# 1/rms of the experts' rows from one-hot products, and spare weight units asked for at other points

## The chip, the cores and the metric

The kernel runs on one core of a Trainium2 chip: TensorE (PE, with PEld for its weight loads), VectorE (DVE), ScalarE (ACT), GpSimd (POOL), SyncE (SP, which issues most of the DMA) and 16 DMA engines between HBM and the on-chip memory. The metric is the device time of one execution in microseconds (us).

## The reference, cut to what matters

One decoder layer for 520 tokens (512 of a prompt, 8 of decoding): a mixer, a mixture of experts, a gate. The change touches the experts' input:

```python
u = rmsnorm(h, g_ffn)              # h * (1/rms of h's row) * g_ffn, per token
# router: softmax over 4 groups, top 1; softmax over its 8 experts, top 2
cw = sum(one_hot(eid, 32) * wk)    # two experts of 32 for each token, with weights
for e in range(32):                # D = 1024, D_FF = 512
    t = silu(u @ w_gate[e]) * (u @ w_up[e])
    y = y + cw[:, e:e+1] * (t @ w_down[e])
h = h + y
```

The weights of the 32 experts are 201 MB of float32, and each token uses two experts. The kernel takes only the rows that belong to an expert.

## The kernel before, in words

**The head** (to about 272 us) is a list of TensorE jobs (`JOBS`): the mixer in 128-column pieces of its weights, the output projection (`wo`), transposes of h into rows (`tp`), the router's logits (`lg`), and at the end `rk` (rank of each token in its expert, by triangular products), `ix` and `iy` (for each expert the list of its tokens, by products of one-hot matrices, helper `placed`) and `tot` (rows of each expert). A job's result lies in one of four pairs of PSUM banks and is read by the engines that `READERS` names. Filler products (`spin`, counts in `SPIN`) stand where TensorE would wait.

**h and its 1/rms.** Rows of h go to a DRAM tensor `h_rows` by POOL (`store_rows`, lines 659 and 660, semaphore `h_stored`). A token has two rows there, each with 512 values of h and, behind them, 16 copies of the token's 1/rms (`HR` = 528 values in a row). The copies are made by ACT (`rstd_rows`, line 845) and written by four DMAs of ACT (lines 849 and 850, `rstd_stored`), 1040 pieces of 64 bytes.

**An expert** has a tile of 64 tokens, 128 rows with both halves of h. POOL gathers them with an indirect DMA (`start_gather`, line 676) into `xg`, two buffers in turn. TensorE transposes them (`rows_t`, line 1733), DVE multiplies by the gain (`evac_rows`, line 1383) and copies the 1/rms of each row out of column 512 of `xg` into `rs` (line 1382). TensorE forms gate and up together (`gate_up`, line 1754), ACT and DVE apply silu, `rs` and the product, TensorE transposes (`hidden_t`, line 1762) and multiplies with the down weights (`down`, line 1771). ACT evacuates, and POOL scatters the result to `y_rows` (line 682). Further tiles for an expert with more than 64 tokens exist (`over`), but no such tile runs in these inputs.

**The weights** come in units of 2 MB, three for an expert: unit 0 and 1 for gate and up, unit 2 for down. There are six slots in `arena` and three spare places (`spare[0..2]`) put together from pieces of other buffers that are free by then, in 5, 4 and 8 pieces. SP asks for them in a fixed order, and every request waits in SP's queue for its own condition. Units 0 to 5 go to the slots, unit 6 to spare 0 during the head. Unit 7 goes to spare 1 (line 485) once `h_stored` is complete. Unit 8 goes to spare 2 once the first gather has landed (`xg_loaded[0]`). Unit 9 goes to the slot of unit 0 when the first half of expert 0's `gate_up` is done (`gu_half`, line 546), unit 10 when all of it is done, unit 11 after its `down`, and so on for all that follow.

**The route.** DVE's `rk` step makes `row_hot` (line 1066, float16) and two subtractions for ACT's exponentials (line 854), then `index` (line 1359), which POOL's gather waits for. Behind the last job of the head, DVE computes the weights `wk` (`route_weights`, lines 1072 to 1084, 14 small operations that wait for the exponentials), and then the first `evac_rows`.

**The tail** (from about 743 us): the last scatter, y read back, the gate, the final norm.

## Time and profile before

| | us |
|---|---|
| median of 3 runs (822.83 to 824.47) | 823.37 |
| the profiled execution, its own time | 825.39 |
| its span | 823.6 |

| engine | busy us | share of the span |
|---|---|---|
| PE | 721.8 | 88% |
| DVE | 288.8 | 35% |
| ACT | 179.6 | 22% |
| POOL | 102.6 | 12% |

All rows come from the profiled execution, whose span is 1.8 us shorter than its own time. 258.39 MB move in all. The page's second part cuts the span in 40 slices of 20.6 us. Busy shares are means over stages with different limits, so a stretch is read by its own rows.

### The profile page before, as it was taken

The numbers are of one execution on the slowest core, as the hardware profiler recorded it, in microseconds if no ns is written. First come the engines' busy times: TensorE is split into PE (matmuls) and PEld (weight loads), VectorE is DVE, ScalarE is ACT, GpSimd is POOL, SyncE is SP. The second block draws the span as 40 slices with busy tenths as digits, with TensorE's granted clock in tenths as the row PEclk, the third lists the DMA queues.
The fourth block names the chain that finished last, engine by engine and source line by source line (L and its number), as shares of the span: only waits on it lengthen the run. The fifth ranks groups of instructions, "written<-read, shape, count | busy, mean of one in ns | idle before, by whom it ended". The sixth has DMA issues, their size and how long they took to land.

```text
span 823.6 us, 11299 instructions
## 1 busy us (share of the span) xinstructions
PE 721.8 (88%) x4520; PEld 450.1 (55%) x4520; DVE 288.8 (35%) x520; ACT 179.6 (22%) x274; POOL 102.6 (12%) x161
## 2 busy tenths in 40 slices
PE   8999999999999888999998887777777777778996
PEld 8989999899998433333333222222222222226775
DVE  5556788676434532010111011011001001005875
ACT  7242312233323010011111010000000000004576
POOL 0500000010001112212121211211211111100000
PEclk9999999999999999999999999999999999999999
DMA  9641225663936799999999999999999999995301
GB/s 347 239 181 53 77 80 210 248 224 98 400 132 217 259 409 416 428 426 425 426 425 426 424 427 427 426 425 428 428 424 429 426 427 426 425 422 218 120 27 77
DMA packets 36457, 258.39 MB, mean 314 GB/s; under 512 B 7905, under 2 KB 8465, under 8 KB 22841
## 3 DMA queue, kind: packets, MB, share of 16 engines
q1 hardware_dynamic: 27248, 237.17, 70.3%
q0 software_dynamic: 7072, 19.07, 6.2%
q10 hardware_dynamic: 2096, 1.56, 0.6%
q8 instruction: 31, 0.51, 0.2%
q14 instruction: 10, 0.07, 0.0%
HBM read 251.04 MB, written 15.14 MB: 323 GB/s over the span
## 4 chain that ended last, share of the span: by engine, by line
PE 53%; DMA 36%; DVE 6%; ACT 3%; issue 2%; SPq 0%; DVEq 0%; POOLq 0%; ACTq 0%
DMA arena<-in_w_exp 33%; PE ps L1560 23%; PE ps L1754 15%; PE ps L1771 5%; PE ps L1885 3%; PE ps L1603 1%; DMA region_q<-in_xt 1%; DVE xh L1423 1%; DVE region_u L1376 1%; DMA region_u<-h_rows,index 1%; DMA region_m<-y_rows 1%; PE ps L1568 1%; DMA y_rows<-region_v,both_cols 1%; PE ps L1762 1%; PE ps L1673 0%
## 5 line engine op out<-in xcount | busy, mean ns | idle before, releaser
L1754 PE MATMUL ps<-arena,region_u 128*64 128x512 f32 x960 | 218.3, 600 | 47.0 <-DMA arena<-in_w_exp 46.0
L1754 PEld LDWEIGHTS ps<-arena,region_u 128*64 128x64 f32 x960 | 66.9, 137 | 196.2 <-issue 124.2
L1372 DVE SCALAR_TENSOR_TENSOR region_u<-ps,small,region_u 128x256 f32<-128x256 f32 x32 | 15.5, 484 | 376.7 <-ACT region_u L858 376.7
L1560 PE MATMUL ps<-u_hi,w_hi 128*128 128x260 f32 x448 | 129.2, 288 | 5.1 <-issue 3.3
L1560 PE MATMUL ps<-u_lo,w_hi 128*128 128x260 f32 x448 | 127.4, 284 | 0.0
L1560 PE MATMUL ps<-u_hi,w_low 128*128 128x260 f32 x448 | 127.3, 284 | 0.0
L1771 PE MATMUL ps<-arena,region_u 128*64 128x512 f32 x480 | 109.6, 598 | 6.1 <-DMA arena<-in_w_exp 2.5
L1560 PEld LDWEIGHTS ps<-u_hi,w_hi 128*128 128x128 f32 x448 | 85.1, 190 | 7.0 <-issue 5.0
L1560 PEld LDWEIGHTS ps<-u_hi,w_low 128*128 128x128 f32 x448 | 85.2, 190 | 0.0
L1560 PEld LDWEIGHTS ps<-u_lo,w_hi 128*128 128x128 f32 x448 | 85.2, 190 | 0.0
L682 POOL DMA_INDIRECT y_rows<-region_v,both_cols x32 | 33.3, 1042 | 367.6 <-ACT region_v L862 367.6
L858 ACT ACTIVATE region_u<-ps,small 128x256 f32<-128x256 f32 x32 | 15.1, 473 | 264.3 <-PE ps L1754 264.3
L1771 PEld LDWEIGHTS ps<-arena,region_u 128*64 128x64 f32 x480 | 33.3, 137 | 63.1 <-issue 54.4
L862 ACT ACTIVATE region_v<-ps 128x512 f32<-128x512 f32 x32 | 19.1, 597 | 158.8 <-PE ps L1771 158.8
L1141 DVE TENSOR_TENSOR w_low<-arena,w_hi 128x1024 fp32r<-128x1024 f32 x35 | 42.7, 1221 | 18.1 <-ACT w_hi L755 17.9
L755 ACT ACTIVATE w_hi<-arena 128x1024 fp32r<-128x1024 f32 x35 | 36.8, 1050 | 24.5 <-PE ps L1560 24.4
L1560 PE MATMUL ps<-mix_lo,w_hi 128*128 128x260 f32 x128 | 36.2, 283 | 0.0
L1762 PE MATMUL ps<-ident,region_u 128*128 128x128 f32 x64 | 13.6, 294 | 25.3 <-DVE region_u L1372 25.2
L1762 PEld LDWEIGHTS ps<-ident,region_u 128*128 128x128 f32 x64 | 7.1, 141 | 50.3 <-DVE region_u L1372 48.0
L676 POOL DMA_INDIRECT region_u<-h_rows,both_cols x30 | 31.3, 1043 | 25.6 <-POOL both_cols L697 25.6
L1885 PE MATMUL ps<-gate_hi,u_hi 128*128 128x512 f32 (+1 forms) x72 | 26.8, 373 | 1.3 <-DVE u_lo L1446 1.3
L1885 PE MATMUL ps<-gate_lo,u_hi 128*128 128x512 f32 (+1 forms) x72 | 26.5, 367 | 0.0
(288 smaller groups left out, 857.6 us busy)
## 6 DMA issues: line engine op xcount, KB each, us to landing
arena<-in_w_exp SPq DMA_DIRECT2D x88, 2048.0 KB, 26.9
arena<-in_w_in SPq DMA_DIRECT2D x35, 512.0 KB, 4.0
region_q<-in_w_exp SPq DMA_DIRECT2D x24, 256.0 KB, 11.1
arena<-in_w_exp SPq DMA_DIRECT2D x8, 512.0 KB, 4.2
arena<-in_w_ple_gate SPq DMA_DIRECT2D x2, 2048.0 KB, 23.6
region_u<-in_xt SPq DMA_DIRECT2D x2, 1040.0 KB, 6.2
arena<-in_state_ret POOLq DMA_DIRECT2D x2, 1024.0 KB, 9.1
xh<-v_few POOLq DMA_DIRECT2D x1, 2048.0 KB, 9.0
```

What stands on the lines that cost most here:

```text
L676: pool.indirect_dma_start(out=xg[b], out_offset=None, in_=h_rows, in_offset=bass.IndirectOffsetOnAxis(ap=at, axis=0), bounds_check=2 * T - ...
L682: pool.indirect_dma_start(out=y_half, out_offset=bass.IndirectOffsetOnAxis(ap=scol[:, b:b + 1], axis=0), in_=out_sb[b], in_offset=None, bo ...
L755: nc.scalar.activation(w_hi[n % WIN_HIGH], w_raw[:, n % WIN_SLOTS, :], ACT.Copy).then_inc(w_hi_ready, 1)
L858: nc.scalar.activation(sg[b], ps[:, 2 + b, 0:256], ACT.Silu, scale=rs[b]).then_inc(out_sem, 1)
L862: nc.scalar.activation(out_sb[b], ps[:, 6 + b, :], ACT.Copy).then_inc(out_sem, 1)
L1141: V.tensor_tensor(w_low[:, n % WIN_SLOTS, :], w_raw[:, n % WIN_SLOTS, :], w_hi[n % WIN_HIGH], ALU.subtract).then_inc(w_lo_ready, 1)
L1372: V.scalar_tensor_tensor(hs[b], ps[:, 2 + b, 256:512], rs[b], sg[b], ALU.mult, ALU.mult).then_inc(out_sem, 1)
L1560: last = mm(halves(out)[:, half, :], w[:, k, :], u[:, cols], start=(k == 0 and s == 0), stop=(k == KD - 1 and s == 2))
L1754: last = mm(ps[side * 64:side * 64 + 64, 2 + b, :], xv[:, k // 4, k % 4, :], rows(k % 4 * 2 + side), start=(k == 0), stop=(k == KD - 1))
L1762: last = tr(ps[:, 4 + b, k * P:(k + 1) * P], hs[b][:, k * P:(k + 1) * P], ident[:, :])
L1771: last = mm(ps[side * 64:side * 64 + 64, 6 + b, :], hv, rows(q * 2 + side), start=(q == 0), stop=(q == 3))
L1885: last = mm(b[:, cols], u[:, k, :], w, start=(k == 0 and i == 0), stop=(k == KD - 1 and i == 2))
```

## The change

The 1/rms no longer travels in the gathered rows. A new job `rs` behind `tot` multiplies the one-hot matrix of the rows, widened to float32 by ACT (`hot_32`), with a table that DVE makes in its `rk` step (`rs_value`, choice times 1/rms). The product is a table of 1/rms by row and expert (`rs_table`), and `evac_rows` takes its column. `h_rows` has 512 values in a row. The 16 copies go to a tensor of their own (`r_rows`), from ACT behind the first pair of experts, and only `over` tiles would read them. The gather doesn't wait for `rstd_stored`. The filler behind `tot` falls from 16 products to 6. SP asks for the first two pieces of unit 7 when POOL has cleared `xg[0]` (`xg_cleared`), for the other two after `h_stored`, and for unit 8 when POOL has reached its second gather (`pool_turn`).

```diff
-    jobs += [("rk", 0), ("ix", 0), ("iy", 0), ("tot", 0)]
+    jobs += [("rk", 0), ("ix", 0), ("iy", 0), ("tot", 0), ("rs", 0)]
...
-HR = 528
-SPIN = (28, 8, 16)
+RW = 16
+SPIN = (28, 8, 6)
...
+        rs_table, rg = region_u[:, moe:moe + NE], region_u[:, moe + NE:moe + NE + RW]
+        hot_32 = region_u[:, 2048:2048 + 2 * NT * ROWS].rearrange("p (n c) -> p n c", c=ROWS)
+        rs_value = both[:, 0:2 * NT * NE].rearrange("p (n e) -> p n e", e=NE)
...
+            sp.wait_ge(xg_cleared, 1)
+            for n in range(2):
+                load_spare(1, n)
             sp.wait_ge(h_stored, 16 * 2 * len(STORES))
-            for n in range(4):
+            for n in range(2, 4):
                 load_spare(1, n)
-            sp.wait_ge(xg_loaded[0], 16)
+
+            sp.wait_ge(pool_turn, 2)
             for n in range(8):
                 load_spare(2, n)
...
+            nc.gpsimd.memset(rg, 1.0).then_inc(xg_cleared, 1)
+            pool.wait_ge(xg_cleared, 3)
             pool.wait_ge(h_stored, 16 * 2 * len(STORES))
-            pool.wait_ge(rstd_stored, 16 * 4)
             pool.wait_ge(index_done, 1)
...
-            act.wait_ge(rows_ready, 1)
-            for half in range(2):
-                act.dma_start(h_full[:, :, half, 512:HR], rstd_rows[:, 0:4, :]).then_inc(rstd_stored, 16)
-                act.dma_start(h_few[:, half, 512:HR], rstd_rows[0:NB, 4, :]).then_inc(rstd_stored, 16)
+            act.wait_ge(hot_done, 1)
+            nc.scalar.activation(hot_32, row_hot, ACT.Copy).then_inc(hot_widened, 1)
...
             pair_of_experts(0, True, False)
+            act.wait_ge(rows_ready, 1)
+            for half in range(2):
+                act.dma_start(r_full[:, :, half, :], rstd_rows[:, 0:4, :]).then_inc(rstd_stored, 16)
+                act.dma_start(r_end[:, half, :], rstd_rows[0:NB, 4, :]).then_inc(rstd_stored, 16)
...
+                    V.tensor_tensor(rs_value.rearrange("p (k t) e -> p k t e", k=2), pick,
+                                    stats[:, 10:15].unsqueeze(1).unsqueeze(3).to_broadcast([P, 2, NT, NE]),
+                                    ALU.mult).then_inc(value_ready, 1)
...
+                elif kind == "rs":
+                    V.tensor_copy(rs_table, b[:, 0:NE]).then_inc(dve_jobs, 1)
...
-                V.tensor_copy(rs[b], xg[b][:, 512:513])
+                if over:
+                    dve.wait_ge(ov["rg"], count * 16)
+                V.tensor_copy(rs[b], rg[:, 0:1] if over else rs_table[:, bass.ds(count - 1, 1)])
...
-                    spin(pair(n + 1), SPIN[2])
+                elif kind == "rs":
+
+                    pe.wait_ge(value_ready, 1)
+                    pe.wait_ge(hot_widened, 1)
+                    last = placed(b[:, 0:NE], hot_32, rs_value)
+                    spin(b[:, 512:1024], SPIN[2])
```

Three places in the order of the instructions follow. On SP, at the end of the head, the requests for unit 7 (`region_v`, `region_m`, two pieces in `region_q`) and unit 8 (seven pieces in `region_q`, one in `region_u`) stand so before:

```order
L485 DMA region_v<-in_w_exp 128x1536 [waits h_stored]
L485 DMA region_m<-in_w_exp 128x1536
L485 DMA region_q<-in_w_exp 128x512 x2
L485 DMA region_q<-in_w_exp 128x512 [waits xg_loaded0]
L485 DMA region_q<-in_w_exp 128x512 x6
L485 DMA region_u<-in_w_exp 128x512
L546 DMA arena<-in_w_exp 128x4096 [waits gu_half]
```

and so with the change:

```order
L491 DMA region_v<-in_w_exp 128x1536 [waits xg_cleared]
L491 DMA region_m<-in_w_exp 128x1536
L491 DMA region_q<-in_w_exp 128x512 [waits h_stored]
L491 DMA region_q<-in_w_exp 128x512
L491 DMA region_q<-in_w_exp 128x512 [waits pool_turn]
L491 DMA region_q<-in_w_exp 128x512 x6
L491 DMA region_u<-in_w_exp 128x512
L556 DMA arena<-in_w_exp 128x4096 [waits gu_half]
```

Nothing changes places here; three requests wait for other events, and unit 9 (the last row) waits for the same one.

On PE, between the index products (`region_m`, 64x32) and the first rows of expert 0 (`ident,region_u`), with the change:

```order
L1609 MATMUL ps<-region_m 64x32 [waits hot_done]
L1609 MATMUL ps<-region_m 64x32 x19
L1609 MATMUL ps<-region_m 64x32 [waits act_jobs]
L1609 MATMUL ps<-region_m 64x32 x9
L1746 MATMUL ps<-region_m,meanw 128x32 [waits act_jobs]
L1746 MATMUL ps<-region_m,meanw 128x32 x4
L1609 MATMUL ps<-region_m,region_u 64x32 [waits hot_widened,value_ready,dve_jobs]
L1609 MATMUL ps<-region_m,region_u 64x32 x19
L1602 MATMUL ps<-ident 128x128 x6
L1760 MATMUL ps<-ident,region_u 128x128 [waits xg_loaded0,dve_jobs,act_jobs]
```

The 20 products with `region_m,region_u` are new, and the filler behind them (`ident`) was x16 and stood directly behind `tot` (`meanw`).

On ACT, from the copies of 1/rms to the first silu, with the change:

```order
L858 ACTIVATE region_m<-stats 128x80 [waits pe_jobs,rstd_done]
L861 ACTIVATE region_u<-region_m 128x640 [waits hot_done]
L865 ACT_TABLE_LOAD
L865 ACTIVATE region_m<-region_m 128x20 [waits lg_ready]
L865 ACTIVATE region_m<-region_m 128x40 [waits lg_ready]
L869 ACT_TABLE_LOAD
L869 ACTIVATE region_u<-ps,small 128x256 [waits gu_done]
```

Before, the four DMA issues stood where the widening copy (128x640) stands now, and the table load behind it waited for nothing.

## Rows read from the trace of the kernel before

**Rows 1.** The page: GB/s in 40 slices of 20.6 us.

```profile
GB/s 347 239 181 53 77 80 210 248 224 98 400 132 217 259 409 416 428 426 425 426 425 426 424 427 427 426 425 428 428 424 429 426 427 426 425 422 218 120 27 77
```

**Rows 2.** A stretch: busy us by engine, granted clock, DMA share, GB/s.

```profile
400.00:500.00 100.00, 89.23 (x408) 31.75 (x406) 11.62 (x28) 11.98 (x23) 16.71 (x28) 1.00 1.01 425
```

**Rows 3.** The chain that ended last: start us, duration us, what.

```profile
272.76 5.11 DMA region_u<-h_rows,index
279.57 8.81 PE ps L1754 x32
...
294.13 6.89 PE ps L1754 x32
...
711.48 26.50 DMA arena<-in_w_exp
```

**Rows 4.** SP's DMA issues from 264 to 330 us: start, duration, line.

```profile
269.07 0.33 SPq L485 DMA_DIRECT2D region_v<-in_w_exp  x1
...
270.39 10.99 SPq L485 DMA_DIRECT2D region_q<-in_w_exp  x9
...
284.96 22.11 SPq L546 DMA_DIRECT2D arena<-in_w_exp  x6
```

**Rows 5.** DMA issues at 160.8, 263.3, 272.8, 274.2, 281.4, 285.0 us; later gathers.

```profile
arena<-in_w_exp SPq DMA_DIRECT2D x1, 2048.0 KB, 7.9
...
h_rows<-xh POOLq DMA_DIRECT2D x1, 512.0 KB, 5.5
...
region_u<-h_rows,index POOLq DMA_INDIRECT x1, 5.1
...
region_u<-h_rows,index POOLq DMA_INDIRECT x1, 4.0
...
region_u<-in_w_exp SPq DMA_DIRECT2D x1, 256.0 KB, 6.5
...
arena<-in_w_exp SPq DMA_DIRECT2D x1, 2048.0 KB, 9.1
...
region_u<-h_rows,both_cols POOLq DMA_INDIRECT x30, 8.9
```

**Rows 6.** DMA queues, 262 to 270 us: packets, MB, share of 16 engines.

```profile
q10 hardware_dynamic: 1088, 0.07, 9.5%
```

**Rows 7.** Instructions from 255 to 300 us: start us, duration us, engine, line.

```profile
257.06 2.31 PE L1704 MATMUL ps<-w_rs,region_u 128*128 128x36 f32 x20
...
264.54 0.56 POOL L665 MEMSET region_u<- 128x528 f32 x1
...
265.56 1.28 ACT L854 ACT_TABLE_LOAD   x1 [2.44 <-issue]
...
268.74 0.49 DVE L1351 TENSOR_TENSOR region_m<-region_m,ps 128x320 f32<-128x320 f16 x1
...
270.66 0.87 PE L1587 MATMUL ps<-region_m 128*64 128x32 f16 x30 [0.27 <-DVE region_m L1066]
...
271.41 0.25 DVE L1359 TENSOR_SCALAR index<-ps,small 128x32 int32<-128x32 f32 x1 [0.60 <-PE ps L1587]
...
271.60 3.82 PE L1580 MATMUL ps<-ident 128*128 128x128 f32 x32
...
272.33 0.16 DVE L1072 TENSOR_REDUCE region_m<-region_m 128x5 f32<-128x20 f32 x1
...
275.20 0.17 DVE L1084 TENSOR_TENSOR wk<-region_m 128x5 f32<-128x5 f32 x1
...
278.00 0.63 PE L1733 MATMUL ps<-ident,region_u 128*128 128x128 f32 x4 [2.58 <-DMA region_u<-h_rows,index]
```

**Rows 8.** The page's groups: busy us, mean ns of one, idle time before.

```profile
L862 ACT ACTIVATE region_v<-ps 128x512 f32<-128x512 f32 x32 | 19.1, 597 | 158.8 <-PE ps L1771 158.8
```

**Rows 9.** Two stretches around expert 0's start, columns as in rows 2.

```profile
278.00:279.00 1.00, 0.63 (x4) 0.39 (x4) 0.24 (x2) 0.00 (x0) 0.00 (x0) 1.00 0.13 16
...
281.00:282.00 1.00, 1.00 (x4) 0.24 (x2) 0.84 (x5) 0.00 (x0) 0.91 (x2) 0.50 0.81 217
```

More of the change, by code:

```diff
@@ L76 @@
                pv="A", st="D", vs="A", lt="D", gc="D", hc="D", gb="D", wo="D", tp="A", lg="D",
-               rk="D", ix="D", iy="D", tot="D", u="D", pa="A", pb="A", pg="A")
+               rk="D", ix="D", iy="D", tot="D", rs="D", u="D", pa="A", pb="A", pg="A")
 JOBS = job_list()
@@ L153, in build @@
     y_rows = nc.dram_tensor("y_rows", [2 * T, D], F32, kind="Internal").ap()
-    h_rows = nc.dram_tensor("h_rows", [2 * T, HR], F32, kind="Internal").ap()
+    h_rows = nc.dram_tensor("h_rows", [2 * T, 512], F32, kind="Internal").ap()
+    r_rows = nc.dram_tensor("r_rows", [2 * T, RW], F32, kind="Internal").ap()
     v_few = nc.dram_tensor("v_few", [1, NB * H * P], F32, kind="Internal").ap()
@@ L159, in build @@
     h_few = h_rows[2 * SEQ:2 * T, :].rearrange("(p n) c -> p n c", n=2)
+    r_full = r_rows[0:2 * SEQ, :].rearrange("(t p n) c -> p t n c", p=P, n=2)
+    r_end = r_rows[2 * SEQ:2 * T, :].rearrange("(p n) c -> p n c", n=2)
     y_tok = y_rows.rearrange("(t k) c -> t (k c)", k=2)
@@ L326, in build @@
         ixf = scratch(NE)
-        rstd_rows = scratch(NT * (HR - 512)).rearrange("p (t c) -> p t c", t=NT)
+        rstd_rows = scratch(NT * RW).rearrange("p (t c) -> p t c", t=NT)
         spare_m = KD * T - 2048
@@ L333, in build @@
         xg, xgT, hs, sg, hT = [], [], [], [], []
-        for lst, width in ((xg, HR), (xgT, 512), (sg, 256), (hs, 256), (hT, 256)):
+        for lst, width in ((xg, 512), (xgT, 512), (sg, 256), (hs, 256), (hT, 256)):
             for _ in range(2):
@@ L380, in build @@
         h_stored, lt_loaded, rows_ready = sem("h_stored"), sem("lt_loaded"), sem("rows_ready")
-        rstd_stored = sem("rstd_stored")
+        rstd_stored, value_ready, hot_widened = sem("rstd_stored"), sem("value_ready"), sem("hot_widened")
         pp_loaded = sem("pp_loaded")
@@ L413, in build @@
         ov = {n: sem("over_" + n) for n in ("w", "xg", "xt", "xgT", "gu", "silu", "hs", "ht", "hT", "down", "out",
-                                            "stored")}
+                                            "stored", "rg")}
         y_loaded = [sem(f"y_loaded{i}") for i in range(2)]
@@ L587, in _ @@
                 sp.wait_ge(over_done, 1)
+            sp.wait_ge(rstd_stored, 16 * 4)
             sp.wait_ge(out_stored[0], 16 * (NE // 2))
@@ L666, in _, with start_gather @@
             nc.gpsimd.memset(xg[1], 0.0).then_inc(xg_cleared, 1)
-            pool.wait_ge(xg_cleared, 2)
+            nc.gpsimd.memset(rg, 1.0).then_inc(xg_cleared, 1)
+            pool.wait_ge(xg_cleared, 3)
             pool.wait_ge(h_stored, 16 * 2 * len(STORES))
-            pool.wait_ge(rstd_stored, 16 * 4)
             pool.wait_ge(index_done, 1)
-            def start_gather(b, at, loaded):
+            def start_gather(b, at, loaded, rows=False):
                 pool.sem_inc(pool_turn, 1)
-                pool.indirect_dma_start(out=xg[b], out_offset=None, in_=h_rows,
+                pool.indirect_dma_start(out=rg if rows else xg[b], out_offset=None, in_=r_rows if rows else h_rows,
                                         in_offset=bass.IndirectOffsetOnAxis(ap=at, axis=0),
@@ L717, in _ @@
             n_over = pool.value_load(over_expert[0:1, OVER:OVER + 1], min_val=0, max_val=OVER)
+            pool.wait_ge(rstd_stored, 16 * 4)
             with pool.If(n_over > 0):
@@ L726, in _ @@
                     start_gather(0, gcol[:, 0:1], ov["xg"])
+                    start_gather(0, gcol[:, 0:1], ov["rg"], True)
                     pool.wait_ge(ov["out"], q + 1)
@@ L1378, in _, with evac_rows @@
             gx = col["gx"].rearrange("p (k h) -> p k h", h=2).unsqueeze(3).to_broadcast([P, 4, 2, ROWS])
-            def evac_rows(b, count, t_done, out_sem):
+            def evac_rows(b, count, t_done, out_sem, over=False):
                 dve.wait_ge(t_done, count)
-                V.tensor_copy(rs[b], xg[b][:, 512:513])
+                if over:
+                    dve.wait_ge(ov["rg"], count * 16)
+                V.tensor_copy(rs[b], rg[:, 0:1] if over else rs_table[:, bass.ds(count - 1, 1)])
                 V.tensor_tensor(xgT[b].rearrange("p (k h r) -> p k h r", h=2, r=ROWS),
@@ L1409, in _ @@
                 with dve.Fori(0, OVER) as q:
-                    evac_rows(0, q + 1, ov["xt"], ov["xgT"])
+                    evac_rows(0, q + 1, ov["xt"], ov["xgT"], True)
                     mult_up(0, q + 1, ov["silu"], ov["hs"])
```

4 lines of the change are left out of this document (2 added, 2 removed).

## The prediction

> **What bounds the kernel now.** I read the page's slices first. From slice 15 (288 us on) to slice 36 the DMA engines move 409 to 428 GB/s [rows 1], and a stretch in the middle shows 425 GB/s at a DMA share of 1.01, while PE is busy 89.23 of 100 us [rows 2]. The expert stage is bound by its 201 MB of weights, and the chain of waits says the same of its last part: a load of 26.5 us, a few products, the next load [rows 3]. Nothing the change does to DVE or PE inside this stage can matter; what matters is when the stream becomes unbroken, and how many bytes are in it.
>
> So I looked for the last hole in the stream. Slices 12 to 14 (226 to 288 us) move 132, 217 and 259 GB/s [rows 1]. The list of SP's issues tells why [rows 4]: unit 7 is asked for at 269.07, its four pieces and the eight of unit 8 end at 281.43 + 0.44, and unit 9 follows at 284.96, released by expert 0's half product. Between them, at 278 to 279 us, the engines move 16 GB/s [rows 9]: unit 7 has landed, unit 8 is only just asked for. From unit 9 on each request waits for PE, which is through a gate and up in 6.89 us [rows 3], while the 6.29 MB of an expert take 14.8 us at 425 GB/s, so PE is ahead of the stream for a while. Unit 9 is therefore the start of the unbroken stream. It lands 9.1 us after its issue, at 294.1, and the last piece of unit 8 lands 6.5 us after 281.4, at 287.9 [rows 4, 5]: unit 9 stood some 3 us behind unit 8.
>
> Two things set its landing: when it is asked for (the chain index, gather, transposes, evacuation, half a gate and up), and what is still in front of it. All times below are of the profiled execution, span 823.6 and own time 825.39; its own time is 2.02 us above the median of 823.37, so I subtract the sum from the median.
>
> **The change part by part.**
>
> *Spare units sooner.* The first two pieces of unit 7 go at the end of the first clearing, 264.54 + 0.56 = 265.1 [rows 7], instead of 269.07: 4.0 us. Unit 8 goes when POOL reaches its second gather, which is issued at 274.2 [rows 5], so at about 274.0, instead of after the first one's landing at 277.9 (272.76 + 5.11 [rows 3]): 3.9 us. With the same spacing and the same slowest landing its last piece is in by 287.9 - 3.9 = 284.0, before unit 9 is asked for. But that doesn't bring unit 9's request forward: the hole moves behind unit 8. What is won is only the queue in front of unit 9. A unit issued at 160.8 landed in 7.9 us against 9.1 [rows 5]: -1.2 us. The bounds are 0 (a gather or a late piece still in front) and -1.2; I take -1.2, as the request for unit 8 is sooner by more than the 3 us.
>
> *The gather of expert 0.* It runs for 5.1 us from 272.76, beside unit 7. The second gather, started 1.4 us later, takes 4.0 [rows 5]. With the change most of unit 7 is in by then and unit 8's first pieces come 1.3 us after the gather's issue. I take 4.5, -0.6 us. Its bounds are 4.0 (-1.1) and 8.9 (+3.8), the median of the 30 later gathers under the full stream [rows 5]; between ends so far apart the two rows of the same place are nearer.
>
> *h's last store* took 5.5 us, to 268.8 [rows 5], and now shares with unit 7. It would have to land after 271.66, where `index` is done (271.41 + 0.25 [rows 7]), to delay the gather; the cover is 2.9 us, and past it a late store costs its excess. At 8.9 us, as a gather in the full stream, that is 272.2, +0.5. I take 0.
>
> *The copies of 1/rms.* The 1040 pieces of 64 bytes move from 263 us to about 307, into the unbroken stream. There they took 9.5% of 8 us of all 16 engines, 0.76 us [rows 6]. That is what they cost if they add to the stream, and 0 if they fit beside other packets; I take half, +0.4. ACT's four issues lie where it waits for expert 2's silu. The Trainium skill (DMA: Bandwidth & Descriptors, Specifications) wants at least 512 bytes in a transfer for line rate, which speaks against the move. By the rule the whole upper end would be paid, and the total would be 0.4 us worse than I put it; the trace agrees that 0.07 MB took as long as 0.3 MB of weights would.
>
> *Shorter rows.* 2080 gathered rows lose 64 bytes each, 0.13 MB, at 425 GB/s -0.3 us; bounds 0 and -0.3 if only bytes count.
>
> *The product `rs`.* The trace has no float32 product of this shape, 20 of 128x64 by 32 columns, two records each. 20 records with 128 weight columns and 36 moving ones take 2.31 us, 115 ns each; 30 float16 records of just this shape take 0.87 us, 29 ns each [rows 7]. So 40 records lie between 1.2 and 4.6 us; I take 60 ns, half of 115 for half the weight columns: 2.4. They start where the fillers did, at 271.6 to 271.8, behind `tot`. What they wait for is there: `row_hot` is done at 270.66, where the index product starts [rows 7], and `hot_32` (128x640, from 597 ns for 512 columns [rows 8] 0.75) ends at 271.4. `rs_value` stands on DVE between two subtractions and `index`; at 0.16 each (like line 1072) and 0.49 (like line 1351 [rows 7]) it ends at 271.3 to 271.5, so `index`, begun at 271.41 before, is late by 0.1 at most. Six fillers at 3.82/16 = 0.24 each [rows 7] end at 275.6, against 275.4 before: PE falls idle at the same time.
>
> Behind `rs` stands what can be late: DVE copies the table at 274.2, then has `route_weights`, 272.33 to 275.37 = 3.0 us before [rows 7]. The exponentials are in time although the table load of 1.28 us [rows 7] now stands behind `hot_32` (271.4 + 1.28 + 0.4 = 273.1). So DVE is free at 277.5. A gather at 272.76 + 4.5 = 277.3 and 0.63 us of transposes [rows 7] ask for it at 278.0: 0.5 us of cover, nothing lost. With 4.6 us for `rs`, DVE is free at 279.7 and the first evacuation 1.7 us late. Below, nothing is gained.
>
> Sum: -1.2 - 0.6 + 0.4 - 0.3 = -1.7 us, which is 821.7.
>
> **The rivals.**
>
> *PE keeps its clock.* The granted clock is 0.50 of 2.4 GHz, the 1.2 GHz level, at 281 to 282 us [rows 9], after PE had idled from 275.4 to 278.0 for the gather. Expert 0's gate and up takes 8.81 us, expert 1's 6.89 [rows 3], and the slow part lies before the half that releases unit 9. If the shorter wait spares the drop, unit 9 is asked for 1.9 us sooner still, and unit 8 is in by then: -3.6, 819.8. For it: the gap shrinks by 0.6 us. Against it: 2 us remain, and a second gap follows the transposes.
>
> *The requests only move the hole.* The gather lands as late as before or DVE is late behind `rs`, which eats the -0.6 and up to 1.7 more: between -1.1 and +0.6, around 822.9. For it: 0.5 us of cover rests on an estimate between 1.2 and 4.6. Against it: half the weight columns.
>
> *Unit 8 crowds the gather: slower.* Its eight pieces are asked for 0.1 to 1.3 us after the gather's issue, where before they waited for its landing. If the gather then takes the 8.9 us of the full stream, everything behind it, unit 9 too, is 3.8 us late: -1.2 + 3.8 + 0.1 = +2.7, 826.1. It decides from a gather of 7.8 us on. For it: 30 gathers out of 30 later ones stand beside weights and have that median. Against it: they stand beside loads of 2 MB, and this one beside pieces of 256 KB and, before, beside 768 KB with 5.1. The Trainium skill (DMA: Bandwidth & Descriptors, Queues, rings and completion order) says that an engine takes turns between its queues, a packet from each; the gather is then slowed by every load beside it, which is this rival's side, and no row here shows it for pieces so small.
>
> **How the numbers follow.** The forecast has a chance of 0.40 with a range of its own from 820.7 to 822.8, the kept clock 0.18, the moved hole 0.26, the crowded gather 0.16. About 0.2% (1.6 us) is what a measurement of this kernel can tell from no change, and the forecast lies on that bound. Faster: half of the forecast, 0.20, all of the kept clock, 0.18, and a quarter of the moved hole (where the clock is kept too), 0.06: 0.44. Slower: the crowded gather but for gathers under 7.8 us, 0.14, and a tenth of the moved hole: 0.17. Same: 0.39. The range from 818.5 to 825.8 leaves out the far ends of the kept clock (0.05) and of the crowded gather (0.08), and holds the bounds of `rs` and of the 64-byte pieces.
>
> **What would show it.** Right: unit 9 lands within 8 us of its issue; SP's row for unit 8 begins near 274; the first gather takes 4 to 5 us; a hole in the stream between unit 8's landing and unit 9's; 425 GB/s as before in the middle. `rs` shows as 40 records in 2.4 us, and DVE's `route_weights` end before the transposes do. Wrong: the first gather takes over 7 us, the first evacuation waits for DVE, or the stage's rate changes.

## The result, and the profile after

| kernel | median us (runs) | against before, with its 95% interval | mean granted clock of the runs |
|---|---|---|---|
| before, beside the changed one | 823.92 (6) | | |
| changed | 827.33 (6) | 1.0041 [1.0022, 1.0059] | 0.9895 |
| changed, in a second series | 828.03 (8) | 1.0065 [1.0044, 1.0086] | 0.9891 |
| before, in that series | 822.85 (31) | | 0.9930 |

The forecast was 821.7 in a range from 818.5 to 825.8, and 0.17 for slower. The kernel is slower by 3.4 to 5.2 us, and the time lies outside the range. The profiled execution is the quickest of the first six: span 822.5, own time 824.36.

In the expert stage nothing moved, as forecast. GB/s in 40 slices, and the same 100 us as in [rows 2] (engines' busy us, granted clock, DMA share, GB/s; 425 before):

```profile
GB/s 348 238 181 57 73 90 224 251 199 127 375 137 224 248 421 405 429 424 426 425 424 427 427 425 426 424 429 425 427 426 427 427 426 425 426 424 221 120 28 77
```

```profile
400.00:500.00 100.00, 89.15 (x406) 31.32 (x404) 11.62 (x28) 11.98 (x23) 16.87 (x27) 1.00 1.01 426
```

The chain that ended last (start, duration) has the same last part as [rows 3]: loads of 26.5 us. What is new in it is the product `rs`, with 3.71 us:

```profile
273.09 3.71 PE ps L1609 x40
...
280.80 7.11 PE ps L1781 x32
...
293.68 6.89 PE ps L1781 x32
...
710.42 26.54 DMA arena<-in_w_exp
```

SP's issues, to be held against [rows 4]: unit 7 starts 4.4 us sooner, unit 8 ends 3.9 us sooner (278.01 after 281.87), and unit 9 is asked for at 284.50 after 284.96:

```profile
264.65 0.33 SPq L491 DMA_DIRECT2D region_v<-in_w_exp  x1
...
267.06 10.25 SPq L491 DMA_DIRECT2D region_q<-in_w_exp  x9
277.36 0.65 SPq L491 DMA_DIRECT2D region_u<-in_w_exp  x1
284.50 12.98 SPq L556 DMA_DIRECT2D arena<-in_w_exp  x4
```

Unit 9 lands 7.7 us after its issue (9.1 in [rows 5]), and the first gather takes 5.0 us (5.1). Each row is a DMA issue with KB and us to landing:

```profile
arena<-in_w_exp SPq DMA_DIRECT2D x1, 2048.0 KB, 7.7
```

```profile
region_u<-h_rows,index POOLq DMA_INDIRECT x1, 5.0
```

From the start of the router's last products to the first evacuation (start, duration, engine, line; in brackets the idle time before and what ended it), to be held against [rows 7]:

```profile
255.36 2.31 PE L1726 MATMUL ps<-w_rs,region_u 128*128 128x36 f32 x20
...
269.45 0.53 PE L1734 MATMUL ps<-region_m,meanw 128*128 128x32 f16 x15
...
270.08 0.49 DVE L1366 TENSOR_TENSOR region_m<-region_m,ps 128x320 f32<-128x320 f16 x1 [2.62 <-PE ps L1734]
...
272.00 0.87 PE L1609 MATMUL ps<-region_m 128*64 128x32 f16 x30
...
272.75 0.25 DVE L1377 TENSOR_SCALAR index<-ps,small 128x32 int32<-128x32 f32 x1 [0.20 <-PE ps L1609]
...
273.02 2.31 PE L1609 MATMUL ps<-region_m,region_u 128*64 128x32 f32 x40
...
275.26 1.60 PE L1602 MATMUL ps<-ident 128*128 128x128 f32 x12
...
276.82 0.19 DVE L1385 COPY region_u<-ps 128x32 f32<-128x32 f32 x1 [3.06 <-PE ps L1609]
...
279.22 0.63 PE L1760 MATMUL ps<-ident,region_u 128*128 128x128 f32 x4 [2.35 <-DMA region_u<-h_rows,index]
...
279.80 0.17 DVE L1099 TENSOR_TENSOR wk<-region_m 128x5 f32<-128x5 f32 x1
280.00 0.15 DVE L1404 COPY small<-region_u 128x1 f32<-128x1 f32 x1
```

Two things are to be seen. From the first 128x36 product to `index` it takes 272.75 - 255.36 = 17.39 us, where [rows 7] have 271.41 - 257.06 = 14.35. The rank products `rk` (L1734) start at 269.45, and DVE has waited 2.62 us for them; before them stand the 28 fillers. The granted clock tells why. These are two stretches of the changed kernel, 12 us from the first 128x36 product and from the first evacuation (L1404) to unit 9's request; the clock is the third column from the end:

```profile
255.36:267.36 12.00, 11.87 (x80) 11.40 (x79) 8.82 (x35) 3.96 (x9) 2.34 (x5) 0.72 0.88 309
280.00:284.50 4.50, 3.70 (x18) 1.35 (x20) 4.03 (x15) 0.00 (x0) 1.40 (x3) 1.00 0.74 268
```

and of the kernel before:

```profile
257.06:269.06 12.00, 11.87 (x119) 11.51 (x118) 9.23 (x36) 5.25 (x10) 2.32 (x4) 1.00 0.83 292
278.76:284.96 6.20, 5.39 (x18) 1.75 (x20) 4.52 (x17) 0.00 (x0) 1.40 (x3) 0.72 0.80 247
```

0.72 over 12 us is 6.7 us at 0.50, the 1.2 GHz level. In this execution the changed kernel lost its clock in the head and kept it in expert 0's gate and up (4.50 us to unit 9's request); before did the reverse (6.20 us). The second thing is at the end of the long fence above: the copy of the 1/rms table (L1385) starts 3.80 us after the first record of `rs`, the routing weights end at 279.97 (L1099), 0.12 us after the transposes. DVE is just in time here; the cover of 0.5 us is used up.

### The profile page after: what moved, and what is told of

Its sections match the earlier page's. It is cut to its first block, busy times and chain, and to the rows that moved or that the text cites. A ratio compares the mean times of both kernels' runs of the same rounds, so it can differ in the third digit from the quotient of the medians.

```text
span 822.5 us, 11373 instructions
## 1 busy us (share of the span) xinstructions
PE 719.3 (87%) x4540; PEld 448.9 (55%) x4540; DVE 289.2 (35%) x522; ACT 180.2 (22%) x275; POOL 102.9 (13%) x162
## 4 chain that ended last, share of the span: by engine, by line
PE 54%; DMA 35%; DVE 6%; ACT 3%; issue 2%; SPq 0%; DVEq 0%; POOLq 0%; ACTq 0%
DMA arena<-in_w_exp 33%; PE ps L1582 23%; PE ps L1781 15%; PE ps L1798 5%; PE ps L1912 3%; PE ps L1625 1%; PE ps L1602 1%; DMA region_q<-in_xt 1%; DVE xh L1445 1%; DMA region_m<-y_rows 1%; DVE region_u L1396 1%; PE ps L1609 1%; PE ps L1706 1%; DMA y_rows<-region_v,both_cols 1%; PE ps L1789 1%
## 5 line engine op out<-in xcount | busy, mean ns | idle before, releaser
L1912 PE MATMUL ps<-gate_lo,u_hi 128*128 128x512 f32 (+1 forms) x72 | 26.5, 367 | 0.0
```

Of the source, the lines that this page charges most:

```text
L1912: last = mm(b[:, cols], u[:, k, :], w, start=(k == 0 and i == 0), stop=(k == KD - 1 and i == 2))
```

## The experiments

Five theories, in the order in which they came up: A, the copy of the `rs` table and the routing weights behind it make DVE late; B, the sooner requests crowd the gather and h's store; C, the 64-byte pieces cost time in the stream; D, the 28 fillers in front of `rk` hold up `index` when the clock is low; E, too few fillers behind `rs` leave PE idle and cost it its clock. All timed kernels in one table:

| kernel | in words | median us (runs) | against before | mean clock |
|---|---|---|---|---|
| route_first | changed, routing weights ahead of the copy | 825.50 (12) | 1.0032 [1.0015, 1.0049] | 0.9902 |
| old_requests | changed, SP's requests as before | 826.68 (12) | 1.0048 [1.0026, 1.0071] | 0.9890 |
| new_requests | before, SP's requests as changed | 824.92 (12) | 1.0024 [1.0005, 1.0044] | 0.9911 |
| both_back | route_first and old_requests together | 824.55 (12) | 1.0013 [0.9995, 1.0030] | 0.9927 |
| few_fill | changed, 18 fillers in front of `rk` | 824.35 (12) | 1.0008 [0.9992, 1.0024] | 0.9886 |
| few_fill_before | before, 18 in front of `rk` | 824.65 (12) | 1.0009 [0.9995, 1.0023] | 0.9888 |
| fill_route | few_fill, route_first, 16 behind `rs` | 823.21 (12) | 0.9998 [0.9980, 1.0016] | 0.9923 |
| mixed | fill_route, unit 8 as before | 823.29 (12) | 1.0001 [0.9986, 1.0016] | 0.9925 |
| full_fill | route_first, 16 behind `rs` | 822.81 (12) | 1.0002 [0.9984, 1.0020] | 0.9930 |
| sooner8 | fill_route, unit 8 sooner still | 825.78 (12) | 1.0026 [1.0014, 1.0039] | 0.9906 |
| sooner8_before | before, 18 in front, requests of sooner8 | 824.77 (11) | 1.0019 [1.0008, 1.0030] | 0.9894 |
| after16 | changed, 16 behind `rs`, nothing else | 823.21 (12) | 0.9998 [0.9980, 1.0016] | 0.9931 |
| before24 | before, 24 behind `tot` | 821.40 (12) | 0.9989 [0.9973, 1.0004] | 0.9943 |
| old16 | both_back, 16 behind `rs` | 823.67 (12) | 1.0009 [0.9991, 1.0027] | 0.9926 |

**The parts undone one by one.** `again` is the changed kernel, `new_requests` the kernel before with only SP's part of the diff.

> The changed kernel once more, with a second profile. In the first profile index came 1.34 us later than before, because the filler of the rk job ran at half clock, and the first gate and up still started only 1.2 us later and at full clock; that execution took 824.36 us, the fastest of six whose median was 827.33. So its trace does not show where the usual 3 us are lost. Theory A (the new chain behind the product rs): DVE's copy of the table waits for PE to be through rs and its fillers, route_weights of 3.0 us comes after it, and the first evacuation after that; in an execution where the clock is low during rs (2.31 us at full clock) and the fillers (1.6 us), the chain grows by up to 3.9 us and the gather no longer covers it. It expects 827 us, runs with a lower mean clock being the slower ones, and in a usual trace the first evacuation waiting for DVE. Theory B (the requests that go out sooner): unit 8 or unit 7 delays the gather or h's store; it expects 827 us with a gather over 7 us in a usual trace. Theory C (the 64-byte pieces in the unbroken stream): 827 us with the loss behind 307 us.

```diff
# route_first
+                if kind == "rs":
+                    route_weights()
...
-            route_weights()
```

> The changed kernel with one edit on DVE: route_weights stands ahead of the copy of rs_table, so its 14 operations run while PE forms rs, and only the copy (0.19 us) is behind the product. Theory A expects most of the loss back: 823 to 824.5 us. Theories B and C expect no difference to the changed kernel, about 827 us.

```diff
# old_requests (new_requests is the reverse, in the kernel before)
-            sp.wait_ge(xg_cleared, 1)
-            for n in range(2):
-                load_spare(1, n)
             sp.wait_ge(h_stored, 16 * 2 * len(STORES))
-            for n in range(2, 4):
+            for n in range(4):
                 load_spare(1, n)
-            sp.wait_ge(pool_turn, 2)
+            sp.wait_ge(xg_loaded[0], 16)
```

> The changed kernel with SP's requests for units 7 and 8 put back to where they stood before (all of unit 7 after h's store, unit 8 after the first gather has landed). Theory A expects it no faster than the changed kernel: 827 to 829 us, since the chain behind rs stays and the 1.2 us in front of unit 9 come back. Theory B expects the time of before, 823 to 824.5 us. Theory C expects 827 us or more.

> The kernel before with nothing changed but SP's requests for units 7 and 8, which go out as in the change. 1/rms still comes with the gathered rows. Theories A and C expect the gain that I forecast for this part alone, -1.2 us: 822 to 823.5 us. Theory B expects the loss here: 826 to 827.5 us.

Measured: 828.03, 825.50, 826.68 and 824.92. Taken alone each part seems to have a share: 2.5 us for the place of the routing weights, 1.4 for the requests (here the intervals overlap), and 2.1 for the requests in the kernel before, between what theories A and C (822 to 823.5) and B (826 to 827.5) expected. Theory C falls. The end comes 538.6 us after unit 9's request before (823.6 - 284.96), 538.0 in the changed kernel and 538.5 in `again`, so the stage behind is no longer; and `after16`, below, has these pieces too and takes the time of before. Theory A has its place in the profile of `old_requests`, where the gather is quick: the transposes (L1756) end at 277.52, and DVE starts the evacuation 1.9 us later, behind the copy (L1381) and the routing weights:

```profile
276.21 0.19 DVE L1381 COPY region_u<-ps 128x32 f32<-128x32 f32 x1 [3.08 <-PE ps L1605]
...
276.89 0.63 PE L1756 MATMUL ps<-ident,region_u 128*128 128x128 f32 x4 [0.64 <-DMA region_u<-h_rows,index]
...
279.38 0.15 DVE L1400 COPY small<-region_u 128x1 f32<-128x1 f32 x1
```

**The head.** `before_again` is the kernel before once more, `after_third` the changed one.

```diff
# few_fill (few_fill_before: the same in the kernel before)
-SPIN = (28, 8, 6)
+SPIN = (18, 8, 6)
```

> The kernel before, once more, for a second profile. Theory D (the granted clock in the head): the changed kernels' profiles all show 0.50 for 3.4 or 6.8 us from about 258 us on, while the 28 fillers stand in front of the products `rk`; there index comes 15.8 to 17.4 us after the first of the 20 products of 128x36. If that fall is caused by the change, this profile shows 1.00 from 256 to 266 us and 14.3 to 14.4 us to index, as the first profile of before did. If it comes and goes by chance in both kernels, a fall here shows 15.8 to 17.4 us. Theories A (DVE late behind rs), B (sooner requests crowd the gather) and C (64-byte pieces) say nothing of it.

> The changed kernel, once more, for its third profile. Five profiles of kernels with rs and 28 fillers show index 17.4 us after the first 128x36 product, three of kernels without rs 14.35 to 15.8. If the change brings the longer low clock with it, 17.4 again; if it comes and goes by chance in both, 14.3 or 15.8 is as likely as 17.4.

> The changed kernel with 18 fillers instead of 28 in front of rk. Theory D: at the low clock the 28 fillers end 1.5 to 2.6 us after the one-hot rows they wait for, and rk, the index and the gather are that late; with 18 the fillers end about 0.3 us after them at most, index comes 15.0 to 15.5 us after the first 128x36 product, and the time falls by 1.5 to 2.5 us, to about 825.5 (from 827.3 to 828.2). Theories A, B, C: what stands behind index is as it was, so the time stays at 827.5 within 0.8; if the fillers had kept the clock up, it gets slower by up to 2.

> The kernel before with 18 fillers instead of 28 in front of rk. Theory D, if the fall of the clock is rarer in before: nothing or at most -0.8 us (822 to 823), since at the full clock the fillers end just as the one-hot rows are ready. If the fall is as frequent in before as in the changed kernel: -1.5 to -2.5 (about 821). If the fillers hold the clock: slower, by 1 to 2.

> The changed kernel with SP's requests as before and the routing weights ahead of the copy behind rs. Theories A and B together: both costs are gone, time that of before within 0.8 us, 822.3 to 823.7. Theory D: neither touches the head, where index comes 17.4 us after the first 128x36 product; the time stays 1.5 to 3 us above before, 824.5 to 826, and this profile shows the low clock from 258 us on.

`before_again` shows 15.76 us to `index`, and a granted clock of 0.86 over the same 12 us; `after_third` shows 14.34 at 1.00, in 823.15 us. So the low clock in the head comes and goes in both kernels. `few_fill_before` takes 824.65, which is not to be told from before (1.0009 [0.9995, 1.0023]). `few_fill` met theory D's number and more, 824.35, with `index` 14.33 us after the first product. In its profile `rk` starts 10.66 us after that product, and no longer 14.09; the second fence has its clock over the 12 us, 0.86:

```profile
255.51 2.31 PE L1726 MATMUL ps<-w_rs,region_u 128*128 128x36 f32 x20
...
266.17 0.53 PE L1734 MATMUL ps<-region_m,meanw 128*128 128x32 f16 x15
...
269.84 0.25 DVE L1377 TENSOR_SCALAR index<-ps,small 128x32 int32<-128x32 f32 x1 [0.20 <-PE ps L1609]
```

```profile
255.51:267.51 12.00, 11.72 (x101) 11.09 (x100) 9.23 (x36) 3.96 (x9) 2.34 (x5) 0.86 0.88 316
```

All 20 profiles together show what the ten fillers cost. With 28 in front, `index` comes 14.35 us after the first product where the clock over the 12 us is 1.00, 15.8 where it is 0.86, and 17.4 where it is 0.72. With 18 it is 14.35, 14.3 to 14.6, and 15.15 (`sooner8_before`). So they cost nothing at the full clock, and up to 2.2 us where the clock is low for longest.

`both_back` came out as theory D said, 824.55, with 17.38 us to `index`. So far D was ahead. It took `full_fill` to show that it is not the whole.

**Fillers behind `rs`, and the company of the gather.**

```diff
# fill_route (also with route_first)          # mixed: fill_route, and
-SPIN = (28, 8, 6)                             -            sp.wait_ge(pool_turn, 2)
+SPIN = (18, 8, 16)                            +            sp.wait_ge(xg_loaded[0], 16)
# no_tail_fill: old_requests with SPIN = (28, 8, 0)
# full_fill: fill_route with SPIN = (28, 8, 16)
# sooner8: fill_route with sp.wait_ge(chosen_done, 1) in place of sp.wait_ge(pool_turn, 2)
```

> The changed kernel with 18 fillers in front of rk, 16 instead of 6 behind rs, and the routing weights ahead of the copy behind rs. Theory D (the 28 fillers at the low clock are the main cost, the copy behind rs and the clock in expert 0's gate and up the rest): index 14.3 us after the first 128x36 product as in few_fill; PE works until about 276 us, so the first gate and up keeps the clock and unit 9 is asked for 4.5 us after the first evacuation starts, as in the changed kernel's first profile, instead of 6.7; time 1.5 to 2.5 us under few_fill, 822 to 823. If the clock falls there all the same: as few_fill, 824.3. Theory B (crowding decides): as few_fill, since SP's requests are the same.

> As fill_route, but unit 8 is asked for after the first gather's landing, as before; unit 7's two pieces stay sooner. Theory B: the first gather takes 3.5 to 3.8 us to the transposes, as in the two kernels with the old requests, instead of 5.2 to 6.1, and the time falls by 1.8 under fill_route, unless unit 8 then stands in front of unit 9. By the two profiles with the old requests the end comes 539.3 and 541.7 us after unit 9's request, 1 to 3 us more than the 538.0 to 538.8 of the others: then the sum is +-1 us against fill_route. Theory D alone: as fill_route.

> The changed kernel with SP's requests as before and no fillers behind rs: what makes the copy of the table late. In three profiles DVE's copy starts 0.8 to 1.5 us after the last record of rs, in two of them just when the 12 filler records behind it end. If the fillers hold it, the copy starts within 0.3 us of the last record here. If the records' ends are too early in the trace, or DVE itself is late, it starts 1.1 to 1.5 us after it again. Theory A needs the copy to be late by its own chain: the first evacuation then starts behind the routing weights, over 1 us after the transposes; with the fillers as the cause it starts 0.4 to 1.2 us sooner.

> As fill_route, but with the changed kernel's 28 fillers in front of rk again (16 behind rs, routing weights first, SP's requests as changed): what the ten fillers alone cost. Theory D: they cost when the granted clock falls in the head; with index 14.3 to 17.4 us after the first 128x36 product from run to run, 1.5 to 2.5 us on the median, 824.7 to 825.7 against 823.2. If the gain of few_fill was something else (the fillers behind rs, the routing weights' place): 823.2 within 0.7.

> As fill_route, but unit 8 is asked for as soon as the one-hot rows are ready (about 11 us after the first 128x36 product, some 5 us before the first gather), not at the second gather. Theory B: its 2 MB need 4.9 us at 425 GB/s, so they are nearly in when the gather starts; the gather takes 3.5 to 4.5 us to the transposes instead of 5.2 to 6.5, unit 9 is asked for 1 to 2 us sooner, and the time falls to 821 to 822.2. If h's last store or the gather then stands behind unit 8: 823.2 to 824.5.

> The kernel before (1/rms still gathered with the rows) with 18 fillers in front of rk and the requests of sooner8: what the requests are worth without rs. Theory B: as for sooner8, 821 to 822.3 against 823.1 for before, and within 0.7 us of sooner8, as then neither the copy behind rs nor the clock in the head decides. If rs still costs its PE and DVE time, this one is 1 to 2 us under sooner8.

`full_fill` has the 28 fillers in front of `rk` and takes 822.81, `fill_route` has 18 and takes 823.21. Theory D, which had 824.7 to 825.7, falls as the sole cause: with 16 behind `rs` the ten fillers in front are worth nothing that shows. `full_fill` differs from `route_first` (825.50) by the ten fillers behind `rs` alone.

`no_tail_fill` has none there, and the copy is as late as with six: 274.81, which is 3.86 us after the first record of `rs`, so the fillers don't hold it:

```profile
270.95 2.31 PE L1605 MATMUL ps<-region_m,region_u 128*64 128x32 f32 x40
...
274.81 0.19 DVE L1381 COPY region_u<-ps 128x32 f32<-128x32 f32 x1 [3.12 <-remote]
```

Its one timed run, 824.13, lies under every run of `old_requests` (825.11 and more), though it has fewer fillers behind `rs`. That goes against theory E; a single run doesn't decide it.

Theory B is right on the gather and wrong on the time. From the gather's issue to the transposes it takes 4.4 us in the mean of nine profiles with unit 8 asked for after its landing (3.5 to 5.6), 5.4 in nine with unit 8 asked for at the second gather (4.7 to 6.5), and 6.5 and 6.6 in the two with unit 8 sooner still. In six of the twenty the transposes wait for fillers or for DVE's copy and not for the gather. Where unit 8 is asked for after the landing, SP's request itself marks it (278.77 in `both_back`): 3.2 to 5.4 us after the issue, 4.0 in the mean; in the other nine the trace has 4.5 to 6.0, 5.1 in the mean. Unit 7 counts as well: with all of it asked for after h's store, the gather lands after 5.1 and 5.4 us where unit 7 was asked for 3.7 and 3.8 us ahead of it (`before`, `few_fill_before`), and after 3.4 and 3.2 us where it was 7.1 and 7.2 (`old_requests`, `both_back`). The quick case, `both_back`, and the slow one, `sooner8`:

```profile
275.55 1.11 POOL L683 DMA_INDIRECT region_u<-h_rows,index  x1 [8.80 <-issue]
...
279.29 0.63 PE L1757 MATMUL ps<-ident,region_u 128*128 128x128 f32 x4 [0.91 <-DVE region_u L1383]
```

```profile
271.43 1.11 POOL L687 DMA_INDIRECT region_u<-h_rows,index  x1 [6.31 <-issue]
...
277.94 0.63 PE L1761 MATMUL ps<-ident,region_u 128*128 128x128 f32 x4 [1.45 <-DMA region_u<-h_rows,index]
```

But `mixed` and `fill_route` take the same time, since the gather's gain is lost again behind unit 8: in `mixed` unit 9 lands 9.1 us after its request and the end comes 541.1 us after it, in `fill_route` 7.5 and 539.6. (`both_back` has 9.4 and 541.7. A difference of 2 us behind unit 9 in one profile says little, though: from its landing to the end it takes 528.3 to 530.4 us in the five profiles without a low clock in the tail near 760 us, and 532.0 to 532.5 in the three with the longest, `mixed`, `both_back` and `sooner8`; the other twelve lie between, 528.7 to 532.1.) `sooner8` lost 2.6 us against `fill_route`, against expectation. Its twin lost 1.9 against before, but only 0.8 of it, by the ratios, is more than `few_fill_before` loses without these requests, and the intervals overlap. In `sooner8` the gather is late and the half product has the low clock: unit 9 is asked for 29.1 us after the first 128x36 product, in `fill_route` 27.3. Unit 8 is all asked for at 272.57, 12.1 us before unit 9, and the stream stands nearly still in between (57 GB/s from 278 to 284 us, 205 in before):

```profile
272.13 0.44 SPq L491 DMA_DIRECT2D region_u<-in_w_exp  x1
284.70 3.76 SPq L556 DMA_DIRECT2D arena<-in_w_exp  x2
```

**The fillers behind `rs` alone.**

```diff
# after16 (old16: the same in both_back)      # before24
-SPIN = (28, 8, 6)                             -SPIN = (28, 8, 16)
+SPIN = (28, 8, 16)                            +SPIN = (28, 8, 24)
```

> The changed kernel with 16 fillers behind rs instead of its 6, nothing else: the part of the change that was costed at nothing, undone. Theory E (fewer fillers behind rs leave PE idle for longer before the first gather lands, and the granted clock falls in expert 0's gate and up more often, 6.2 instead of 4.5 us from the first evacuation to unit 9's request): 825.2 to 826, that is 2 to 2.5 us under the changed kernel; the routing weights' place keeps a share of 2. If E is wrong and the routing weights' place or the requests decide: 827.3 to 828.

> The kernel before with 24 fillers behind tot instead of 16, which end at about 277.2 instead of 275.4, 0.8 us before the transposes. Theory E: the fall of the clock to 0.50 at 280 us goes, unit 9 is asked for 4.5 to 5 us after the first evacuation instead of 6.2, and the time falls by 0.5 to 1.7 us, to 821.2 to 822.4. If the fall comes without regard to the fillers: 822.9 within 0.5.

> The changed kernel with SP's requests as before, the routing weights ahead of the copy, and 16 fillers behind rs. Theory E: 1 to 1.7 us under both_back (824.55), 822.9 to 823.5, and against full_fill (822.8, the same but for SP's requests) the difference is what the requests are worth: theory B says this one is faster by up to 1 us, as the gather takes 3.7 instead of 5.5 us; the later unit 8 in front of unit 9 says slower by 1 to 3.

`after16` undoes one number of the diff and takes the whole loss back: 823.21, 0.9998 [0.9980, 1.0016] of before. That is 2 us under what theory E expected (825.2 to 826), which had left the routing weights a share. `before24` is at 821.40, where theory E put it, though its interval reaches to no change. `old16` is within 0.9 us of `full_fill`, so with the fillers in place the requests are worth nothing that shows, and after16 against `full_fill` says the same of the routing weights' place.

The profiles show what the fillers do. In `again` they end at 279.10, PE stands until the transposes at 282.38, and once more until gate and up; the second fence has the clock of the two stretches as above:

```profile
277.50 1.60 PE L1602 MATMUL ps<-ident 128*128 128x128 f32 x12
...
282.38 0.63 PE L1760 MATMUL ps<-ident,region_u 128*128 128x128 f32 x4 [3.27 <-DMA region_u<-h_rows,index]
...
283.95 0.20 PEld L1781 LDWEIGHTS ps<-arena,region_u 128*64 128x64 f32 x4 [1.18 <-DVE region_u L1405]
```

```profile
257.61:269.61 12.00, 11.87 (x80) 11.40 (x79) 8.73 (x35) 3.96 (x9) 2.34 (x5) 0.72 0.88 308
283.14:289.34 6.20, 5.39 (x18) 1.75 (x20) 4.51 (x17) 0.00 (x0) 1.40 (x3) 0.72 0.33 117
```

In `after16` the fillers reach to the transposes, and in `before24` too:

```profile
276.73 3.84 PE L1602 MATMUL ps<-ident 128*128 128x128 f32 x32
...
280.40 0.60 PE L1760 MATMUL ps<-ident,region_u 128*128 128x128 f32 x4
...
282.40 0.20 PEld L1781 LDWEIGHTS ps<-arena,region_u 128*64 128x64 f32 x4 [1.63 <-DVE region_u L1405]
```

```profile
258.45:270.45 12.00, 11.87 (x94) 11.40 (x93) 8.91 (x35) 3.96 (x9) 2.34 (x5) 0.86 0.86 305
281.59:286.09 4.50, 3.69 (x18) 1.35 (x20) 4.03 (x15) 0.00 (x0) 1.40 (x3) 1.00 0.63 225
```

```profile
271.19 5.60 PE L1580 MATMUL ps<-ident 128*128 128x128 f32 x48
...
276.63 0.60 PE L1733 MATMUL ps<-ident,region_u 128*128 128x128 f32 x4
...
278.18 0.20 PEld L1754 LDWEIGHTS ps<-arena,region_u 128*64 128x64 f32 x4 [1.18 <-DVE region_u L1383]
```

```profile
255.15:267.15 12.00, 11.87 (x93) 11.46 (x92) 8.91 (x35) 5.25 (x10) 2.32 (x4) 0.86 0.82 290
277.37:281.87 4.50, 3.69 (x18) 1.35 (x20) 4.04 (x15) 0.00 (x0) 1.40 (x3) 1.00 0.88 241
```

Over all 20 profiles: where PE stood for 0.9 to 1.8 us in sum between the last filler (in `no_tail_fill` the last record of `rs`) and gate and up, the transposes left out, expert 0's half product was granted 1.00 (seven of seven), and unit 9 was asked for 4.5 us after the evacuation. Where PE stood for 2.4 to 4.9 us it was granted 0.58 to 0.72 (twelve of thirteen), and that took 6.0 to 7.1 us; the one exception is the first profile of the changed kernel, 3.3 us and 1.00. The Trainium skill (TensorE: Matmul & The Clock Gate, HAM oscillation) names gaps on PE as what brings the low clock into a kernel; nineteen of these twenty agree, though it tells of one long wait, and here it was mostly two shorter ones with the transposes between them.

This may also be why A and B seemed to have a share; it rests on one profile of each. In `old_requests` PE stands for 0.65 us ahead of the transposes and for 2.66 behind them, waiting for DVE. In `route_first` DVE is in time, but the gather is slow, and PE stands for 2.68 us ahead. Only with both undone does the sum fall to 1.8 us, and `both_back` keeps the clock.

## Why the prediction was wrong

**The step that failed** is the last one on the product: "Six fillers at 3.82/16 = 0.24 each [rows 7] end at 275.6, against 275.4 before: PE falls idle at the same time." On this the loss of ten fillers was costed at nothing. With 16 again, and all else of the change in place, the time is that of before: 4.1 us under the changed kernel's first median, 4.8 under its second (each beside its own runs of before: 0.9998 after 1.0041 and 1.0065). The premise was nearly right. PE's wait up to gate and up, as defined above, is 3.3, 4.2 and 3.4 us in the three profiles of the changed kernel and 3.5 and 2.6 in the two of before. The conclusion was wrong, since it took PE's wait and its clock as given. What the ten fillers are worth is the wait that they would have filled, and in the changed kernel this is most of it: 1.4 us are left in `after16`.

A second step failed beside it: `index` was to be "late by 0.1 at most". `rs_value` did not delay it, but the low clock in the head did: it came 17.4, 17.4 and 14.35 us after the first 128x36 product in the three profiles of the changed kernel, 14.35 and 15.8 in the two of before. The sum has no term for the clock in the head.

**Where the loss against before sits** is shown in part. From the first 128x36 product to unit 9's request it takes 29.1, 31.7 and 27.9 us in the three profiles of the changed kernel, 27.9 and 28.4 in the two of before. Expert 0's gate and up is no place of the loss, since before loses its clock there as well; what 16 fillers give back there (1.7 us) pays for other costs of the change. `after16` against `before24`, both with 1.00 in that stretch and measured side by side, puts those at 823.21 - 821.40 = 1.8 us, though the two intervals overlap. The gather beside unit 8 (1.0 us) and the late copy (0 to 1.7 us) are the places that the traces offer for it; no timed run shows a price for either with 16 fillers in place. The other part is the head. The time to `index` is 17.4 us in five of seven profiles with 28 fillers in front and six or none behind, and 14.3 to 15.9 in seven of seven with 16 or more behind; the means are 16.7 and 15.6. By these, 1.8 + 1.1 = 2.9 of the 3.4 to 5.2 us can be placed, as an estimate.

The granted clock over whole runs, which is on record for many more executions than the profiles, points the same way. 2 x (1 - clock) x time is the time at the 1.2 GHz level: 17.3 us in the mean of 15 runs of the changed kernel, 11.9 in 139 of before, 11.4 in `after16`. Among the runs of before each of these us goes with 0.37 us of time (correlation 0.87), so the 5.4 us more are worth about 2.0 of the 4.2 us between the means. It doesn't say where: the profiles have low stretches near 11, 58 and 760 us as well. And it isn't all: `few_fill` and `few_fill_before` spend 18.8 and 18.4 us at that level and are not to be told from before. By these figures the two remedies differ: ten fewer in front make the low clock cheap in the head, ten more behind make it rarer. The changed kernel, with 28 in front and six behind, has it often and at a high price.

**What stays open:** why fillers that come after `index` should go with a longer low stretch ahead of it; nothing that the change moves runs before that stretch, and `sooner8_before` has 0.72 there with 16 behind. Why `new_requests`, with 16 fillers behind `tot`, is slower than before by 2.1 us (1.0024 [1.0005, 1.0044]), while `after16` and `full_fill`, with the same requests, are not. Six to twelve runs show most of these times; the head shows only in the profiles, one to three of a kernel, and those of the changed kernel differ by 6.5 us in their own times.

**Unit 9 lands in 7.9 us**: right, 7.7. The gain was booked as 1.2 us, and none of it shows at the end: from unit 9's request it takes 538.0, 538.5 and 538.6 us in the changed kernel, 538.6 and 538.0 in before.

**The gather**, -0.6: not borne out. It landed after 5.0, 6.0 and 4.6 us, in before after 5.1 and 4.2. That unit 7 is further along does help, as the quick gathers with the old requests show, but unit 8 at the second gather makes it 1.0 us longer in the mean. The crowding rival had the direction, and its +3.8 was far too much; even with unit 8 in front of the gather it was +2.1.

**h's last store**, 0 with a bound of +0.5: the bound held. In `new_requests` the gather starts 1.88 us after `index`, before 1.35; in the changed kernel `index` is later anyway, and it is 1.30.

**The 64-byte pieces and the shorter rows**, +0.4 and -0.3: nothing of either shows in the time from unit 9 on.

**The product `rs`**: 40 records in 2.31 us, forecast 2.4. But what counts is when DVE can read it, and the copy starts 3.1 to 3.9 us after the first record, in seven profiles with DVE idle ahead of it. The duration was right for the records and wrong for the result, near the upper bound of 4.6. The cover of 0.5 us was gone: where the routing weights stand behind the copy, the first evacuation starts 0.1 to 1.9 us after the transposes' end (before: 0.1). On the median that cost nothing that shows (`full_fill` against `after16`, 822.81 and 823.21).

**The kept clock** was a rival with the right price, 1.9 us forecast and 6.20 - 4.50 = 1.70 measured. Its condition was put wrong: the wait was down to 0.9 to 1.8 us wherever the clock was kept behind fillers, and a wait shorter by 0.6 us, 2.9, would still lie among those that lost it. `before24` has the kept clock without the change, at 1.7 us under before, with an interval that reaches to no change.

## What to carry to other kernels

A row of fillers is worth the wait that it fills before the next real product: count that wait again when a change moves what the product waits for, and cost fillers taken away by the stretch behind them at the low clock. Fillers ahead of a product on the critical path have a price too, which shows only where the clock is low. When several edits each take a loss back and do not add, look for a thing that they share, as the wait before gate and up here, or for two that must meet; set the clock over all runs beside the few profiles, and take more than one profile before calling a stretch's clock normal. For a product that another engine reads, take the time from its first record to the reader's start in a trace, not the span of its records.

## What was not expected of the hardware

- Twenty float32 products with 64 weight columns and 32 moving ones show 40 records in 2.31 us, but DVE's waiting copy starts 0.8 to 1.6 us after the last of them, with or without fillers behind. Behind the 20 float16 records of the same shape `index` starts after 0.2 us (272.00 + 20 x 0.029 = 272.58, and 272.75, in the long fence above). The trace doesn't tell whether PE ends later than its records or the release is late.
- Asking for a 2 MB unit ahead of the gather, from 3.1 and 3.6 us before its issue on, made it the slowest of all, 6.4 and 6.5 us to its landing (`sooner8`, `sooner8_before`).
